# Prompt attention: eight absorbed-query matmuls after each piece of the first two wide score units, instead of one block of sixteen behind the third unit

## What is computed

```python
def attn_scores(q_nope, q_pe, k_nope, k_pe):
    s = jnp.einsum("bqhd,bkhd->bhqk", q_nope, k_nope).astype(F32)
    s = s + jnp.einsum("bqhr,bkr->bhqk", q_pe, k_pe).astype(F32)
    return s * SCALE
...
    # attend_prompt, per block of 128 queries
    sc = attn_scores(qn, qp, k_nope, k_pe)
    sc = jnp.where(kpos[None, :] <= qpos[:, None], sc, NEG_INF)
    p = jax.nn.softmax(sc, axis=-1)
    return jnp.einsum("bhqk,bkhd->bqhd", p.astype(v.dtype), v)
...
    # attend_sample: keys expanded from cached latents, page by page
    k_nope, v = expand_kv(ckv.astype(q_nope.dtype), lp)
    sc = attn_scores(q_nope, q_pe, k_nope, kpe.astype(q_pe.dtype))
```

## Time and profile before

| | us |
|---|---|
| median of 3 executions | 1824.62 |
| lowest, highest | 1824.05, 1825.17 |
| the profiled execution | 1825.16 |
| span of the profiled execution, first to last instruction | 1823.30 |
| TensorE busy in that span | 1754.5 (96%) |
| VectorE busy | 1029.8 (56%) |
| ScalarE busy | 526.8 (29%) |
| GpSimd busy | 389.0 (21%) |

### The profile page before, as it was taken

One profiled execution on the slowest core, in us unless ns is written; L12 is line 12 of the kernel. 1 busy time (PEld: TensorE's weight loads), 2 busy tenths in 40 slices (PEclk: granted clock), 3 DMA queues, 4 the chain that ended last, 5 costly groups with the idle time before them and its releaser, 6 DMA issues.

```text
span 1823.3 us, 27190 instructions
## 1 busy us (share of the span) xinstructions
PE 1754.5 (96%) x10268; PEld 1555.5 (85%) x10268; DVE 1029.8 (56%) x1675; ACT 526.8 (29%) x1042; POOL 389.0 (21%) x262
## 2 busy tenths in 40 slices
PE   7999899999999999899999999999999999999998
PEld 6999786666888888778899899898898998998886
DVE  5475886775898898856434424324334334244543
ACT  5202355654544444644311111111111111112111
POOL 2204594221555556513200000000000000000000
PEclk9999998999999999999999999999999999999999
DMA  6301000001422222120111111111111111112011
GB/s 200 118 5 42 14 1 0 1 25 32 139 64 54 70 68 70 50 81 1 47 47 47 46 46 46 46 46 46 31 40 45 46 46 46 46 70 78 30 47 39
DMA packets 108947, 91.89 MB, mean 50 GB/s; under 512 B 25571, under 2 KB 97792, under 8 KB 108845
## 3 DMA queue, kind: packets, MB, share of 16 engines
q1 hardware_dynamic: 106851, 89.63, 16.3%
q10 hardware_dynamic: 2002, 1.03, 0.2%
HBM read 84.73 MB, written 6.26 MB: 50 GB/s over the span
## 4 chain that ended last, share of the span: by engine, by line
PE 80%; DVE 7%; POOL 4%; ACT 3%; issue 3%; SPq 2%; DMA 1%; ACTq 0%; POOLq 0%; DVEq 0%
PE ps L1966 22%; PE ps L1968 22%; PE ps L1967 22%; POOL stats L753 2%; PE ps L2378 2%; PE ps L2208 1%; PE ps L538 1%; SPq L626 1%; PE ps L1973 1%; DVE arena L1791 1%; PE ps L2165 1%; DVE arena L1419 1%; PE ps L2270 1%; PE ps L2161 1%; PE ps L2167 1%
## 5 line engine op out<-in xcount | busy, mean ns | idle before, releaser
L1966 PE MATMUL ps<-h_hi,w_hi 128*128 128x384 f32 (+1 forms) x1056 | 346.1, 328 | 0.0
L1967 PE MATMUL ps<-h_lo,w_hi 128*128 128x384 f32 (+1 forms) x1056 | 345.9, 328 | 0.0
L1968 PE MATMUL ps<-h_hi,w_lo 128*128 128x384 f32 (+1 forms) x1056 | 345.9, 328 | 0.0
L1888 DVE TENSOR_TENSOR gate_s<-gate_s,ps 128x384 f32<-128x384 f32 (+1 forms) x66 | 35.1, 532 | 339.1 <-PE ps L1968 339.1
L887 POOL TENSOR_TENSOR arena<-arena,mhalf 128x32 f32<-128x32 f32 x32 | 176.4, 5513 | 128.9 <-DVE arena L1795 128.9
L532 POOL TENSOR_TENSOR stats<-stats,mhalf 128x1 f32<-128x1 f32 (+1 forms) x18 | 9.9, 553 | 888.7 <-DVE stats L522 888.7
L1967 PEld LDWEIGHTS ps<-h_lo,w_hi 128*128 128x128 f32 x1056 | 198.9, 188 | 0.5
L1966 PEld LDWEIGHTS ps<-h_hi,w_hi 128*128 128x128 f32 x1056 | 198.9, 188 | 0.5
L1968 PEld LDWEIGHTS ps<-h_hi,w_lo 128*128 128x128 f32 x1056 | 198.9, 188 | 0.0
L1900 DVE TENSOR_TENSOR arena<-arena,ps 128x512 f32<-128x512 f32 x187 | 128.5, 687 | 122.6 <-PE ps L1968 108.4
L1966 PE MATMUL ps<-cw_hi,pT_hi 128*128 128x288 f32 x512 | 162.0, 316 | 9.9 <-DVE pT_lo L1706 5.6
(11 more groups left out here) (328 smaller groups left out, 3574.5 us busy)
## 6 DMA issues: line engine op xcount, KB each, us to landing
arena<-in_cache_ckv SPq DMA_DIRECT2D x128, 128.0 KB, 2.1
w_raw<-in_w_gate SPq DMA_DIRECT2D x22, 512.0 KB, 4.0
w_raw<-in_w_up SPq DMA_DIRECT2D x22, 512.0 KB, 5.2
arena<-in_x_prompt SPq DMA_DIRECT2D x16, 512.0 KB, 5.3
w_uk<-in_w_down SPq DMA_DIRECT2D x11, 512.0 KB, 3.5
w_uv<-in_w_down SPq DMA_DIRECT2D x11, 512.0 KB, 4.2
gw_raw<-in_w_in SPq DMA_DIRECT2D x8, 512.0 KB, 6.3
w_out<-in_w_out SPq DMA_DIRECT2D x1, 4096.0 KB, 13.5
```

The costliest lines, as they stand in the source:

```text
L1888: ch.link(nc.vector.tensor_tensor(gate_s[:, c], gate_s[:, c], ps[:, 2 * b + 1, 0:n], ALU.mult))
L1966: mm(out, left[0], right[0], start=start, stop=False)
L1967: mm(out, left[0], right[1], start=False, stop=False)
L1968: return mm(out, left[1], right[0], start=False, stop=stop)
```

## The change

In the changed kernel the sixteen matmuls of the absorbed queries are taken out from behind `scores(0, 0)`. A function `absorb(heads)` issues them for given heads, and `scores` calls it after each piece, before the causal matmul. Units (1, 0) and (1, 1) have two pieces each, and each piece is followed by the four matmuls (eight records) of two heads. `abs_done` is counted by the last of them, which now stands ahead of the causal matmul of unit (1, 1). Nothing is added or removed, and the other engines' programs are unchanged.

```diff
+            def absorb(heads):
+                for h in heads:
+                    for k in range(LC):
+                        last = mm(ps[:, 5 + k, h * NS:(h + 1) * NS], w_ukT[:, h, k * P:(k + 1) * P], qT_s[0:DN, h, :], start=True, stop=True)
+                if NH - 1 in heads:
+                    last.then_inc(s_("abs_done"), 1)
+
-            def scores(g, k):
+            def scores(g, k, absorbing=((), ())):
                 c, s, i, hp = unit_of(g, k)
...
                         last = mm(out, q[1], kh_r, start=False, stop=b <= i)
+                    absorb(absorbing[a // 4])
                     if b > i:
                         last = mm(s_view(g, k)[:, i * P:(i + 1) * P], ident_r, causal_r, start=False, stop=True)
                 last.then_inc(s_("scores_done"), 1)
...
             pe.wait_ge(s_("self_place"), 3)
-            scores(1, 0)
+            scores(1, 0, ((0, 1), (2, 3)))
 
             pe.wait_ge(s_("self_ready"), 1)
-            scores(1, 1)
+            scores(1, 1, ((4, 5), (6, 7)))
             scores(0, 0)
-            for h in range(NH):
-                for k in range(LC):
-                    last = mm(ps[:, 5 + k, h * NS:(h + 1) * NS], w_ukT[:, h, k * P:(k + 1) * P], qT_s[0:DN, h, :], start=True, stop=True)
-            last.then_inc(s_("abs_done"), 1)
             for k in range(STEPS):
```

## The result

The changed kernel took 1836.16 us in the median of its first four executions (1831.05 to 1837.00), the kernel before 1824.34 (1821.90 to 1825.17): a ratio of 1.0049, 95% interval 1.0028 to 1.0071. It is slower, beyond the 0.2% that I took as the limit of what can be told, and the median lies above my range of 1824.0 to 1831.0. A second measurement of the same program gave 1.0039 (1.0023 to 1.0055).

A forecast was written before the change was run, and what follows sets the result against it. TensorE, busy for 96% of the span, was taken as the bound. Later scores (0, 1) +1.20, clock fall 0, low level's reach +1.7 and loop 0 gave +2.9 us: 1824.62 to 1827.5 us, range 1824.0 to 1831.0.

The forecast's parts named there:

- the likeliest case: Opening of prompt attention: the pause comes, the low clock reaches some way into the first steps; +0.5 to +3.6 us.
- step 1: Absorbed queries between score pieces in the opening run at full clock: 3.45 us for 32 records, bounds 3.0 and 4.9.
- step 5: After the pause, the low clock reaches into wide_T(0) and the scores behind it: +1.7 us, bounds 0 and 2.9.
- step 4: Pause makes the clock fall around 300; scores (0, 1) and (1, 2) take 3.89 us as before, difference 0.
- Step 2: Behind unit (1, 1) the same chain runs; PE idles some 2.6 us, scores (0, 1) start 1.20 us later.
- Step 3: ACT's copy to q_abs, 1.02 us behind the exponentials, is done before wide_T(0) asks for it: adds nothing.
- rival B: First steps after the pause: the low clock outlasts unit (1, 3), +5.4 to +6 us, over 0.2% slower; chance 0.35.
- Step 6: Loop behind the opening: the shift is passed on, not swallowed; 0, with bounds -1.7 and +1.7 us for the clock.

The follow-up runs named there:

- fill_both: Changed kernel plus one float32 matmul ahead of the queries' last turns and three in the pause behind scores (0, 0); median 1827.4 us, ratio 1.0016.
- dense_twice: Kernel before plus two float32 matmuls, ahead of the queries' last turns and between scores (0, 0) and the block; median 1825.9 us, ratio 0.9999.
- block_mid: Changed kernel with the 16 absorbed-query matmuls as one block between units (1, 0) and (1, 1); median 1829.87 us, ratio 1.0030.
- dense_resume: Changed kernel plus one float32 matmul ahead of the first piece of scores (1, 2), right behind the pause; median 1828.73 us.
- fill_pause: Changed kernel plus three float32 matmuls in the pause behind scores (0, 0); median 1827.75 us, ratio 1.0023.
- after_again: Changed kernel, unchanged, measured and profiled once more; median 1831.5 us of ten executions.

## Why the prediction was wrong

The time lies outside the range, and the likeliest case was within 0.2%. The pause and the chain behind it were right. The cost of the absorbed queries in their new place (step 1) and the reach of the low level (step 5) were not, and the fall of the clock came where step 4 put it for another reason than the one given.

**Step 1** failed, in two terms. It took 4.9 us up to the end of unit (1, 1) in place of 3.45. The eight changes between 96-row and 64-row weights were missing from my sum, about 1.3 us. The other 0.1 is the pace, 0.112 us a record and not 0.108: of the 22 and 12 loads that I counted in the earlier trace rows, 34 for 32 records, two stand in both stretches. I had even let the bounds go down, for a load hidden behind the piece ahead. One such change stood in the trace of before (unit (0, 0) to the block) and I did not price it. And "mixed evenly with score pieces they should leave it so" was wrong in all three profiles: the clock fell at 296.2 and 296.4 among the mixed pieces and at 298.96 right behind them.

**Step 2** was right. The chain behind unit (1, 1) is the one forecast, the pause 2.44 us (2.4 to 2.8 forecast). The start of scores (0, 1) was 1.47 us later than forecast, which is step 1's error alone.

**Step 3** was right: ACT's copy started at 301.63 and held nobody.

**Step 4** was right in its number, PEclk 0.50 after the pause and 3.90 us for scores (0, 1) and (1, 2), but not in its reason. I had the pause bring the clock down. It was down 0.4, 4.5 and 4.6 us before the pause began in the three profiles, and in fill_both it fell at nearly the same place, 298.72, with the pause filled. That the number came out is luck.

**Step 5** is the term that was mis-sized. I put the low level's reach at +1.7 us with bounds of 0 and 2.9. It reached into unit (1, 4), 17.1 us long, and cost 3.9 us in the profile; two more profiles had 20.5 us. What I had wrong is that unbroken work of PE brings the clock back, as it seemed to before: here PE was busy throughout from 302.37 to 305.78 and the clock stayed down. I had this as rival B, with +5.4 to +6, and the profiled execution came out at +5.9; I gave it 0.35. The bound of 2.9 came from low stretches of before that had ended early, though one of them, busy throughout, had already lasted 6.8 us. As to the turns of `wide_T(0)`, the rule of the Trainium skill ("TensorE: Matmul & The Clock Gate", Part 4: PE-mode transpose) stays open. The low level did last through them here, as by that rule, but through the scores behind them as well. Against the rule, in dense_twice the clock came back at 305.79, right after a stretch most of whose work was eight turns and a pause, and it had not come back after the stretch of scores ahead of it:

```profile
298.96:302.38 3.42, 3.42 (x10) 1.97 (x8) 0.29 (x1) 1.02 (x1) 0.00 (x0) 0.50 0.00 0
302.38:305.79 3.41, 2.87 (x12) 2.17 (x10) 1.59 (x3) 0.44 (x3) 0.00 (x0) 0.50 0.00 0
```

**Step 6** was right in kind: the shift was passed on, and one low stretch at a pair's end went, within the 1.7 us that I had left open.

**What no step had** is the spread. I took the clock's course in one profiled execution for the kernel's own. Of 15 executions 6 were above 1834, and three of the first four, so that the median of four stands 4.6 us above that of 15. The runs of the changed kernel with and without a filler ahead of the opening (none of 12 above 1833, and 6 of 15) point to the fall of the clock around the pause before the opening: with the absorbed queries behind it, it could last for 34 us, or for 27 until a filler ended it. No profile of the changed kernel itself caught such an execution; it was seen in those of block_mid and dense_resume, both above 1836 and both with a mean clock of 0.987, where the six have 0.986 to 0.988. That this is what makes the six is argued, not shown. Without that group the changed kernel is at 1831, about 0.3% over before.

## What to carry to other kernels

A small block of thin matmuls that stands behind a producer may be the cover for another engine's chain: before moving it ahead of the producer's end, look at what PE would then wait for. Where the clock has fallen, the stretch behind the fall has to be priced by how long the low level may hold on under just that work, and here it held for 14 us after a pause of 2.3 to 2.6 us although PE was busy, and for 17 to 34 us in all. A clock that is low behind a pause need not have fallen in it: see whether the record of the clock changes before the pause or in it. And where matmuls of 64 and of 96 rows alternate, each change has its price (0.16 us here), so that one block is cheaper than four (by 1.6 us at 1.2 GHz).

## What was not expected

- Added work made the kernel faster: three matmuls in a pause took 3.8 us off the median (fill_pause against after_again). One behind it cut the low stretch behind the pause from 14 to 5 us (dense_resume).
- The clock fell while PE was busy, and not in the pause, in nine of the ten profiles in which it fell between the opening's start and scores (0, 1), in fill_both with the pause filled. Filling the pause shortened the low level, it did not prevent the fall there.
- At 1.2 GHz the opening with its scores and absorbed queries left the clock low for as long as 22 us (dense_resume), with PE busy for 19.8 us of them.
- The kernel before scatters over 14.9 us (1818.8 to 1833.6 in 105 executions), ordered by the mean granted clock. The first three executions had shown 1.1 us of that.
